# Two transformer blocks on one core: the query up-projection moved ahead of the gate blocks, attention outputs turned inside the last head steps, and gathered banks emptied as they fill

## What is computed

```python
z = rms_norm(x) @ w_in      # qa, ka, va, cq, ckv, k_rope, g_a, g_b
q1, q2, k1, k2 = rope(...)  # differential attention ("DA"), 8 heads
oa = rms_norm(o1 - lam * o2, da_subln) * 0.8 ; y_a = merge_heads(oa) @ w_proj_a
qb = rms_norm(cq) @ w_uq    # query up-projection, 8 x (128 + 64 roped)
kv = rms_norm(ckv) @ w_ukv ; kb_rope = rope(k_rope)   # latent attention ("MLA")
merged = sigmoid(g_a) * y_a + sigmoid(g_b) * y_b
...
hid = silu(u @ w1) * (u @ w3) * gates ; y += hid @ w2  # per expert
```

## Time and profile before

| | |
|---|---|
| median of 3 runs | 990.62 us (990.29 to 992.16) |
| profiled execution, time | 991.64 us |
| profiled execution, span on the core | 989.6 us |
| mean granted clock of TensorE | 0.981 |
| TensorE busy | 929.7 us, 94% |
| VectorE, ScalarE, GpSimd busy | 687.2, 524.6, 245.5 us |
| HBM | 197.41 MB read, 202 GB/s over the span |

### The profile page before, as it was taken

One profiled execution on the slowest core, in us unless ns is written; L12 is line 12 of the kernel. 1 busy time (PEld: TensorE's weight loads), 2 busy tenths in 40 slices (PEclk: granted clock), 3 DMA queues, 4 the chain that ended last, 5 costly groups with the idle time before them and its releaser, 6 DMA issues. The chain is left out here.

```text
span 989.6 us, 12787 instructions
## 1 busy us (share of the span) xinstructions
PE 929.7 (94%) x4415; PEld 749.5 (76%) x4415; DVE 687.2 (69%) x944; ACT 524.6 (53%) x830; POOL 245.5 (25%) x228
## 2 busy tenths in 40 slices
PE   7998999889999999999989999997998979999995
PEld 5886776678786888888768897685777758888774
DVE  5877477846757577777675444996577866786983
ACT  6655666655356344444464456544344455675661
POOL 3776046499522011110038000023100100000001
PEclk9998999989999999999999999998999989999998
DMA  8656746445565899998636665343235274997961
GB/s 259 212 159 215 233 139 199 162 156 181 175 214 153 295 298 320 311 312 269 205 100 208 182 201 196 94 148 107 85 134 171 80 237 151 311 344 244 320 227 42
DMA packets 117254, 199.19 MB, mean 201 GB/s; under 512 B 6433, under 2 KB 64993, under 8 KB 116945
## 3 DMA queue, kind: packets, MB, share of 16 engines
q1 hardware_dynamic: 111296, 176.78, 54.8%
q0 software_dynamic: 5904, 21.72, 6.7%
HBM read 197.41 MB, written 2.62 MB: 202 GB/s over the span
## 5 line engine op out<-in xcount | busy, mean ns | idle before, releaser
L1582 DVE TENSOR_TENSOR w_lo<-raw,w_hi 128x1024 fp32r<-128x1024 f32 x220 | 287.1, 1316 | 136.7 <-ACT w_hi L1014 134.3
L1014 ACT ACTIVATE w_hi<-raw 128x1024 fp32r<-128x1024 f32 x220 | 229.5, 1059 | 115.0 <-PE lin L2468 79.3
L2466 PE MATMUL lin<-w_hi,a_hi 128*128 128x512 f32 (+2 forms) x600 | 239.7, 400 | 3.5 <-DVE w_lo L1582 1.8
L2468 PE MATMUL lin<-w_hi,a_lo 128*128 128x512 f32 (+2 forms) x600 | 232.7, 388 | 0.0
L2467 PE MATMUL lin<-w_lo,a_hi 128*128 128x512 f32 (+2 forms) x592 | 229.6, 388 | 0.0
L2466 PEld LDWEIGHTS lin<-w_hi,a_hi 128*128 128x128 f32 x600 | 114.3, 191 | 29.9 <-issue 3.0
L2468 PEld LDWEIGHTS lin<-w_hi,a_lo 128*128 128x128 f32 x600 | 114.2, 190 | 23.8
L887 POOL TENSOR_SCALAR stat<-stat 128x2 f32<-128x2 f32 (+1 forms) x31 | 10.8, 347 | 489.0 <-ACT idk_t L1139 426.3
L2467 PEld LDWEIGHTS lin<-w_lo,a_hi 128*128 128x128 f32 x592 | 112.9, 191 | 21.0
L934 POOL TENSOR_SCALAR rows<-rows,c_col 128x1024 f32<-128x1024 f32 x16 | 49.0, 3064 | 2.2 <-POOL mod L935 1.5
L953 POOL DMA_DIRECT2D arena<-in_w_ada_dram x32 | 16.9, 528 | 123.9 <-DVE mod L1676 123.3
(11 more groups left out here) (498 smaller groups left out, 1853.1 us busy)
## 6 DMA issues: line engine op xcount, KB each, us to landing
raw<-in_w_in_dram SPq DMA_DIRECT2D x76, 512.0 KB, 4.3
arena<-in_w_ada_dram POOLq DMA_DIRECT2D x32, 512.0 KB, 5.5
raw<-in_w_ffn_gate_dram SPq DMA_DIRECT2D x22, 512.0 KB, 5.1
raw<-in_w_ffn_up_dram SPq DMA_DIRECT2D x22, 512.0 KB, 5.9
raw<-in_w_ffn_down_dram SPq DMA_DIRECT2D x22, 512.0 KB, 4.2
rows<-in_w_ada_dram SPq DMA_DIRECT2D x16, 512.0 KB, 4.0
raw<-in_w_o_dram SPq DMA_DIRECT2D x16, 512.0 KB, 4.2
raw<-in_w_gate_dram SPq DMA_DIRECT2D x16, 512.0 KB, 4.0
```

Of the source, the lines that this page charges most:

```text
L1014: act.activation(w_hi[:, s, :], raw[:, s, :], ACT.Copy).then_inc(hi_ready, 1)
L1582: dve.tensor_tensor(w_lo[:, s, :], raw[:, s, :], w_hi[:, s, :].bitcast(F32), ALU.subtract)\
L2466: pe.matmul(dst, l_hi, r_hi, start=start, stop=False)
L2468: return pe.matmul(dst, l_lo, r_hi, start=False, stop=stop)
```

## The change

uq is put ahead of in8 to in11, and in11 ahead of ukv. In the DA loop the fills are one each in steps 0 to 5, and none at the beginning of later ones; the query rotations go from steps 7 and 8 to 3 and 5, the shared key's from ahead of the latents' turn to steps 2 and 4. cl.2 is turned behind the next unit. oa.0 is turned in step 8, oa.1 in step 9, oa.2 and oa.3 behind the loop with a unit between them, and one unit stands between kr and mq0; MLA's step 0 gives up its unit. DVE splits xo1's last unit before it adds xo0. Among the experts, ACT and DVE empty gather1 before other work, ACT's scaling of expert 0 is split around gather2, the Silu table comes behind it, the paired split of units 10 and 11 comes behind gather2 instead of ahead of gather1, and the additions to `x` go from the position of expert 3 to positions 1 and 2.

```diff
-DA_FILL = [(1, 1, 1)] * 5 + [(1, 2, 1), (0, 0, 1)] + [(0, 1, 1)] * 3
-MLA_FILL = [1] * (HEADS + 2)
+DA_FILL = [(1, 1, 1)] * 6 + [(0, 1, 1)] * 3 + [(0, 1, 0)]
+MLA_FILL = [0] + [1] * 9
...
-ROTATED_AT = (7, 8)
+ROTATED_AT = (3, 5)
+KEY_ROTATED_AT = (2, 4)
...
-    order = [(f"in{n}", DK, "act") for n in (0, 1, 2, 3, 6, 7, 4, 5, 8, 9, 10)]
+    order = [(f"in{n}", DK, "act") for n in (0, 1, 2, 3, 6, 7, 4, 5)]
     order += [(f"uq{n}", QR // P, "act") for n in range(3)]
+    order += [(f"in{n}", DK, "act") for n in range(8, 12)]
     order += [(f"ukv{n}", KVR // P, "act") for n in range(4)]
-    order += [("in11", DK, "act")]
...
# ScalarE
             turned_hi("cl.1", b_hi, 2, 2)
+            fill(1)
             turned_hi("cl.2", b_hi, 4, 1)
-            fill(1)
...
                 fill(DA_FILL[i][0])
+                if i == HEADS + 1:
+                    turned_hi("oa.1", a_hi, 2, 2)
...
+                if i == HEADS:
+                    turned_hi("oa.0", a_hi, 0, 2)
                 fill(DA_FILL[i][2])
-            for g in range(4):
-                turned_hi(f"oa.{g}", a_hi, 2 * g, 2)
...
+            turned_hi("oa.2", a_hi, 4, 2)
+            fill(1)
+            turned_hi("oa.3", a_hi, 6, 2)
+            rope_out(0)
+            rope_out(1)
             turned_copy("kr", ...
+            fill(1)
...
-            act.activation(st("route", 30, 1), st("neg_half", 0, 1), ACT.Silu)
-            act.wait_ge(gates_known, 1)
-            for t in range(NT):
+            def y_first_gated(t):
...
-            for kt in (1, 3, 5):
-                split_to(u + AHEAD - 1 + kt // 2)
-                side(0, kt)
+            side(0, 1)
+            y_first_gated(0)
+            side(0, 3)
+            y_first_gated(1)
+            act.activation(st("route", 30, 1), st("neg_half", 0, 1), ACT.Silu)
+            split_to(u + AHEAD)
+            side(0, 5)
             split_to(u + AHEAD + 2)
...
# VectorE
-            for t in range(NT):
-                rotate1(lat[:, t, QR + KVR:C_W]..., t, 1)
             fill(2)
-            for g, nk in ((0, 2), (1, 2), (2, 1)):
-                turned_lo(f"cl.{g}", b_hi, b_lo, 2 * g, nk)
+            turned_lo("cl.0", b_hi, b_lo, 0, 2)
+            turned_lo("cl.1", b_hi, b_lo, 2, 2)
+            fill(1)
+            turned_lo("cl.2", b_hi, b_lo, 4, 1)
...
+                if i in KEY_ROTATED_AT:
+                    t = KEY_ROTATED_AT.index(i)
+                    rotate1(lat[:, t, QR + KVR:C_W]..., t, 1)
...
-            for g in range(4):
-                turned_lo(f"oa.{g}", a_hi, a_lo, 2 * g, 2)
+            turned_lo("oa.2", a_hi, a_lo, 4, 2)
+            fill(1)
+            turned_lo("oa.3", a_hi, a_lo, 6, 2)
+            fill(1)
...
-            fill(0, "xo0")
+            fill(3)
             u_next = BLOCKS["MOE"][1]
             split_to(u_next)
+            fill(0, "xo0")
...
+            side(0, 1)
             by_choice_of(1, ...
...
-            for kt in (1, 3, 5):
-                split_to(u + AHEAD - 1 + kt // 2)
-                side(0, kt)
+            side(0, 3)
+            split_to(u + AHEAD)
+            side(0, 5)
...
+                if p in (1, 2):
+                    t = p - 1
+                    dve.wait_ge(y_first_out, 2 * NT)
+                    dve.wait_ge(freed["act"], TURNS["ad11"][2])
+                    step(dve.tensor_tensor(y_first[t], y_first[t], mod[:, 5 * D:6 * D], ALU.mult))
+                    step(dve.tensor_tensor(x[:, t, :], x[:, t, :], y_first[t], ALU.add))
...
-                if p == LAST_DENSE:
-                    ...
# TensorE
-            turn_rows("cl", lambda t, k: col(lat[:, t, :], k), 5)
+            for g in range(2):
+                turn_all(f"cl.{g}", ...
             fill(1)
+            turn_all("cl.2", [col(lat[:, t, :], 4) for t in range(NT)])
...
+                if i == 0:
+                    pairs_freed("cl.2")
                 fill(DA_FILL[i][0])
+                if i == HEADS + 1:
+                    turn_heads(1)
...
+                if i == HEADS:
+                    turn_heads(0)
                 fill(DA_FILL[i][2])
...
+            turn_heads(2)
+            fill(1)
             pe.wait_ge(freed["dve"], TURNS["dao7"][2])
-            turn_rows("oa", lambda t, k: head_out[:, t, k, :])
+            turn_heads(3)
             pe.wait_ge(roped, 1)
-            pe.wait_ge(evac["act"], BLOCKS["ukv3"][4])
+            turn_rope(0)
+            turn_rope(1)
...
+            fill(1)
+            pe.wait_ge(evac["act"], BLOCKS["ukv3"][4])
             turn_mq(0)
             turn_mq(1)
```

More of the change, by code:

```diff
@@ L178, in plan_turns @@
             order.append((f"dap{h - 1}", "act"))
+        if h == HEADS + 1:
+            order.append(("oa.1", "dve"))
         if 2 <= h:
             order.append((f"dao{h - 2}", "dve"))
-    order += [(f"oa.{g}", "dve") for g in range(4)]
+        if h == HEADS:
+            order.append(("oa.0", "dve"))
+    order += [("oa.2", "dve"), ("oa.3", "dve")]
     order += [(f"mr{g}", "act") for g in range(2)]
@@ L1525, in _ @@
             split_to(u + 4)
[L1526 to L1528 removed]
+            def y_first_gated(t):
                 if t == 0:
+                    act.wait_ge(gates_known, 1)
                     act.wait_ge(y_first_done, 1)
@@ L1932, in _ @@
                     j.then_inc(freed["dve"], 1)
+                if i == HEADS:
+                    turned_lo("oa.0", a_hi, a_lo, 0, 2)
                 fill(DA_FILL[i][2])
```

27 lines of the change are left out of this document (11 added, 16 removed).

## The result

The changed kernel takes **979.8 us** (median of four runs, 978.6 to 981.7) where the kernel before took 991.38 beside it (median of four, 990.3 to 992.2). The ratio is 0.9886, 95% interval 0.9870 to 0.9902. That is 11.6 us less; 16.5 were forecast, to 974.1, and the range of 967 to 984 holds the result. The profiled execution took 978.6 us (span 976.7) against 991.64, so the two traces differ by 13.0 us (12.9 in their spans), and it is these 13.0 that can be followed in them.

What follows compares the result with a forecast made beforehand. PE, busy 94% of the span, was taken as the bound. Terms -5.2 - 4.0 - 4.0 - 1.4 - 1.2 - 0.7 = -16.5 against 991.64 gave 975.1, or 974.1 for the median; range 967 to 984 us.

Steps and rivals of the forecast that it cites:

- Latents' turn: At cl.0 to cl.2, before DA: the 3.34 us wait and low clock behind it go; -5.2 us, bounds -3.3 and -5.7.
- DA loop: Second half of the loop: fuller fills and moved rotations leave 1.5 of 5.5 us idle; -4.0, bounds 0 and -5.
- rival C: Waits pass to the next bank, rotations cost as much, low stretches stay; DA gives 0; 982.5 us, chance 0.16.
- From DA to MLA: oa turns to MLA's first matmuls: 3.1 of 7.1 us waits and low clock stay; -4.0, bounds -1.5 and -5.5.
- Queues: SP's weight loads behind POOL's early rows: PE arriving 4 us earlier is hidden by 8 us of lead; 0.
- rival B: POOL's queue holds SP's weight loads and paces the MLA loop, returning 4.0 us; 978.1 us, chance 0.12.
- xo1 and additions: Splitting xo1 before adding xo0 saves 1.4 us; moving the additions to x among the experts saves 0.7 us.
- Gathers: Expert 1's hidden rows come 4.1 us sooner, stall moves, low clock returns 2.9; -1.2, bounds +0.5 and -4.1.
- The clock: Low stretches go at the latents and behind DA; behind the moved gather stall it falls again for 6 to 7 us.

Runs made afterwards that it cites:

- POOL cut: POOL's two instructions per early row of w_ada_2 cut to 8 of 1024 columns: 971.6 us on the changed kernel, 987.72 us on the kernel before.
- The third attempt: Changed kernel with ACT's split before the exponentials, oa.0 behind a unit, gathers reordered, gather5's bank emptied before the split of units 16 and 17: 969.14 us, fastest.

## Why the prediction was right, and where it was wrong

**The result** lies in the range, but the sum was 3.5 us too good against the trace (16.5 for 13.0), and that it was not further off is in part luck: the DA loop and the way behind it gave 4.6 us less than forecast, the gathers 1.8 us more.

**Latents' turn: right.** -5.0 for -5.2; the 3.34 us wait and the low clock are gone, and the turn behind cl.2 waits 0.50, as said. Confirmed by itself on the kernel before.

**DA loop: wrong, and this step failed.** -0.8 for -4.0. I wrote that the idle time arises "where the fills are thin" and that moving one unit and the rotations would leave 1.5 of 5.5 us. Neither move alone is worth anything beside POOL's rows as they are: putting the fills back cost nothing (1.3 us less to dap7), nor did putting the rotations back. What the runs put in its place: the late steps with two units are set by the circle maxima, exponentials, ACT's split, DVE's split, mix, split (9.6 us), and POOL's early rows lengthen it. Breaking the circle at ACT's split gave 4.1 us with every unit in its place; silencing POOL gave 4.4. Either is enough, since PE's own work is then the longer. I had seen POOL's long form at the rotation and priced it only there; it meets other DVE instructions with two inputs in SBUF too, the mix above all. My reason was not all wrong: with POOL cut in both kernels the change gives 3.1 us. So the failed step is that the 5.5 us were put down to fills and rotations alone: 2.2 of them were POOL's, and in the new order POOL takes 4.4. Of rival C this is the DA part, at nearly its full size (0.8, the bound having been 0).

One reading behind that term was wrong as well. I said that step 8's block waited 1.73 us at 183.59 because DVE's first rotation was late. ACT, before the change:

```profile
179.89 0.37 ACT L1157 ACTIVATE probs<-sco,stat 128x128 f32<-128x128 f32 x1 [2.86 <-DVE stat L1741]
...
182.44 1.09 ACT L1064 ACTIVATE arena<-lin 128x512 f32<-128x512 f32 x2
```

The copy for which PE waits (182.44) stands behind the exponentials, and these began at 179.89, as soon as DVE had the maxima; the rotation began behind the maxima, at 179.78, and held up neither. That moving it gave nothing fits with this.

**From DA to MLA: right in its mechanism, one wait overlooked.** -2.6 for -4.0. The clock held at 1.00, and the waits of mr0 and mr1 (0.68 and 1.01) came for 0.7 and 1.7. What is missing is the wait of oa.0 at 183.76, 1.1 us, which I had at nothing. It is as long with POOL cut (0.94) and with the circle broken (1.09), so it belongs to oa.0's new place, and it went when oa.0 was turned behind a unit.

**Queues, priced at 0: right as a sum, not in its parts.** SP's waits for POOL are 45.1 us, as before, and between 90 and 300 us ACT never waited for a landing. But rival B happened in another shape: PE came 8 us sooner into the blocks behind MLA, POOL's last row ended only 3 us sooner, and DVE's merge of pb0 met it there. That wait (1.26 us at 260.68) ate what MLA had gained. I had followed POOL's queue only as a holder of loads, not as a neighbour of DVE.

**xo1 and additions: right.** The wait of 1.40 is gone; the block itself is 1.7 us shorter (from the last turn before it), -0.9 with what the clock did between 490 and 730 us. The additions -1.0 for -0.7.

**Gathers: mechanism right, its size off.** The stall moved to the two places named: 1.68 for 1.75 and 2.02 for 2.5. The mis-sized term is what the low clock gives back: I took a stretch of 6 to 7 us as in the earlier trace rows, it was 3.41 us long, and 1.4 us came back for 2.9. Net -3.0 for -1.2. The third attempt showed that the moved stall could be had as well, once the bank's lo part went ahead of every split that was not yet due.

**The clock.** Two of the three low stretches went, that at the gathers became shorter, and a new one of 3.41 us stands behind u's turn (from 492.35), where PE was idle for 2.09 us; before it was idle for 2.00 there, and the clock held. The idle time alone does not decide it: the clock fell behind the same 2.00 us in the kernel before with POOL cut (from 497.82), and it held behind the same 2.09 us in the fastest kernel above. In some experiments one came back behind the DA loop. By the Trainium skill (TensorE: Matmul & The Clock Gate, A second HAM failure mode), which has small idle moments between groups of matmuls throttle the clock, none was sure to go; the trace of the changed kernel does not agree for the two early ones, and those of the experiments do in part. When the clock falls behind such a wait is left open by these runs.

## What to carry to other kernels

Before you move work between the steps of a loop, follow one step around all engines and see which chain has its length; if that is longer than PE's work, another order of PE's units helps little (0.8 us here), and one instruction taken out of the chain (here a split made before it was due, 4.1 us) does. Price an engine that "isn't the bottleneck" by what it does to its neighbours: look for instructions of one form with two durations and for what ran beside the long ones. When a stall moves, look for what stands ahead of the late instruction and is not due yet, and repeat until there is nothing.

## What the runs showed of the hardware

DVE and POOL excluded each other, in both directions. A DVE instruction with two SBUF inputs that began during POOL's 128x1024 TENSOR_TENSOR ended its own time after POOL's end: the second split of the row at 121.45 took 3.4 us for 1.22, and L1659 2.02 for 0.69. Against POOL's TENSOR_SCALAR such an instruction was held only until about 1 us after POOL's start (the two of the mix at 170.92: 1.61 us for 0.74), and a split that began 1.9 us after such a start was not longer (1.21 us from 172.97). Reductions from PSUM beside the addition were not longer (two in 1.02 us from 144.09). The Trainium skill (SBUF — State Buffer, SBUF: two separate sides) calls the pair of ports an exclusive lock, which whoever starts first keeps for the whole instruction. By that rule, the trace of the TENSOR_TENSOR agrees, to 0.2 us; that of the TENSOR_SCALAR does not, since DVE went on 2 us before its end.

The low stretches of PE's clock were 3.41 or 6.83 us long in all these kernels but for the last one of each. With the same code around them they came or not: one of 3.41 us stands from 182.71 in the first attempt at the gathers, whose DA loop is that of the changed kernel, and none there in the changed kernel. At half rate that is up to 1.7 us a piece, or 3.4 for the long ones, and the reason why pieces of the span say more here than two medians.
